# Two out-projections of an encoder by columns instead of rows, norm factors by logarithm and exponential

## The reference

```python
def rmsnorm(x, g, eps=EPS):
    xf = x.astype(jnp.float32)
    xf = xf * lax.rsqrt(jnp.mean(xf * xf, axis=-1, keepdims=True) + eps)
    return (xf * g.astype(jnp.float32)).astype(x.dtype)

# attention, behind the heads; o is (B, S, 8 heads, 128)
o = rmsnorm(o, subln_g, SUBLN_EPS) * (1.0 - lam_init)
o = o.reshape(B, S, D) * jax.nn.silu(z)
return o @ w_out
# Fourier
return (f * jax.nn.silu(z)) @ w_out
# trunk
h = rmsnorm(x, attn_norm);  x = x + diff_attn_branch(h, ...)
h = rmsnorm(x, fnet_norm);  x = x + fourier_branch(h, ...)
return rmsnorm(x, final_norm)
```

## Time and profile before

| | |
|---|---|
| median of 3 runs | 2958.13 us (2956.58 to 2959.44) |
| the profiled execution | 2956.63 us |
| its span in the profile | 2954.8 us, 1.8 us less |
| mean granted TensorE clock | 0.98 of full |
| TensorE busy | 2830.8 us, 96% of the span |
| VectorE, ScalarE, GpSimd busy | 1813.1, 1742.5, 1551.8 us |
| oa | about 2044 to 2302 us |
| of | about 2734 to 2955 us |

### The profile page before, as it was taken

How to read it: one execution, slowest core, us unless ns; L and a number is a source line. 1 busy time by engine, 2 the same in 40 slices (tenths; PEclk the granted TensorE clock), 3 DMA queues, 4 the chain that set the end, 5 groups by cost and what they waited for, 6 DMA issues and landing times. The chain is left out here.

```text
span 2954.8 us, 41608 instructions
## 1 busy us (share of the span) xinstructions
PE 2830.8 (96%) x15126; PEld 2485.9 (84%) x15126; DVE 1813.1 (61%) x2402; ACT 1742.5 (59%) x3126; POOL 1551.8 (53%) x988
## 2 busy tenths in 40 slices
PE   5999999999899999999999999998999899999898
PEld 4999999999688888888888888886788899886687
DVE  7678768766477767677777777776885200441322
ACT  6777777767477777777777777775443311322321
POOL 4556655645265666666566666666563310230642
PEclk8999999999899999999999999999999999999899
DMA  3564554447452314141414131123564522555752
GB/s 112 188 195 139 173 173 149 148 147 204 119 174 79 105 31 107 36 109 36 107 30 109 37 100 46 33 88 115 187 206 165 170 89 78 159 169 200 256 194 98
DMA packets 281815, 374.02 MB, mean 127 GB/s; under 512 B 22923, under 2 KB 258507, under 8 KB 276140
## 3 DMA queue, kind: packets, MB, share of 16 engines
q1 hardware_dynamic: 281484, 371.23, 40.6%
q0 software_dynamic: 128, 0.13, 0.0%
HBM read 258.04 MB, written 125.97 MB: 130 GB/s over the span
## 5 line engine op out<-in xcount | busy, mean ns | idle before, releaser
L1285 DVE TENSOR_REDUCE pa_half_max<-pa_score 128x1 f32<-128x1024 f32 x512 | 624.0, 1219 | 310.4 <-PE pa_score L1055 310.3
L1209 ACT ACTIVATE pa_p<-pa_score,pa_neg_max 128x1024 f32<-128x1024 f32 x512 | 567.8, 1111 | 69.9 <-DVE pa_neg_max L1291 69.8
L1111 PE MATMUL pa_o_acc<-pa_wt,pa_vv 128*128 128x256 f32 x2048 | 507.8, 380 | 1.5 <-ACT pa_o_out_s L1248 1.4
L206 PE MATMUL ia_acc<-ia_xh,ia_wh 128*128 128x384 f32 x1344 | 454.3, 338 | 33.3 <-DVE ia_xl L675 16.0
L451 POOL TENSOR_TENSOR ia_w_sums<-ia_raw 128x512 f32<-128x512 f32 x240 | 334.5, 1397 | 256.5 <-PE ia_acc L208 234.8
L1051 PE MATMUL pa_score<-pa_ka,pa_qa 128*128 128x512 f32 x1024 | 452.1, 442 | 16.3 <-ACT pa_p L1209 8.8
L207 PE MATMUL ia_acc<-ia_xl,ia_wh 128*128 128x384 f32 x1344 | 452.2, 336 | 0.0
L208 PE MATMUL ia_acc<-ia_xh,ia_wl 128*128 128x384 f32 x1344 | 452.1, 336 | 0.0
L1187 ACT ACTIVATE pa_wt<-pa_turned 128x512 f32<-128x512 f32 x512 | 306.2, 598 | 229.1 <-PE pa_turned L1085 221.6
L1055 PE MATMUL pa_score<-pa_kb,pa_qb 96*128 96x512 f32 x1024 | 422.1, 412 | 0.0
L1111 PEld LDWEIGHTS pa_o_acc<-pa_wt,pa_vv 128*128 128x128 f32 x2048 | 367.6, 190 | 46.0 <-ACT pa_o_out_s L1248 3.1
(11 more groups left out here) (286 smaller groups left out, 5245.5 us busy)
## 6 DMA issues: line engine op xcount, KB each, us to landing
ia_raw<-attn_w_in SPq DMA_DIRECT2D x48, 1024.0 KB, 6.3
qk_hi<-ia_hi SPq DMA_DIRECT2D x96, 192.0 KB, 4.9
qk_lo<-ia_c SPq DMA_DIRECT2D x96, 192.0 KB, 2.8
pa_ka<-qk_hi SPq DMA_DIRECT2D x32, 512.0 KB, 8.8
fl_slices<-normed SPq DMA_DIRECT2D x26, 512.0 KB, 6.7
ia_h<-x_cols SPq DMA_DIRECT2D x24, 384.0 KB, 4.1
v<-ia_c SPq DMA_DIRECT2D x48, 192.0 KB, 5.6
attn_gate<-ia_c SPq DMA_DIRECT2D x48, 192.0 KB, 2.0
```

What stands on the lines that cost most here:

```text
L206: pe.matmul(out, a_hi(k), b_hi(k), start=first and n == 0, stop=False)
L1111: mm = pe.matmul(acc, vv[:, k], wt[:, g % 2, k], start=k == 0, stop=k == NB - 1)
L1209: act.activation(dst[:, half * HALF:(half + 1) * HALF], score[:, (4 * q + j) % RING].rearrange("p a b -> p (a b)"), ACT.Exp, bias=neg_max[ ...
L1285: dve.tensor_reduce(half_max[:, q % 2, n, half:half + 1], score[:, (4 * q + j) % RING].rearrange("p a b -> p (a b)"), AX_X, ALU.max).then_ ...
```

## The change

`project_rows` becomes `project_out`, in which everything behind the product stays in columns.

- The weights are the stationary operand and the branch moves: matmuls of 256 columns (a pair's tokens), 1728 per stage. A pair has four quarters `r` of two blocks of output features; `acc` is four PSUM banks, each zeroed by a matmul at the beginning, the first pair being accumulated on these zeros.
- The residual comes in columns (`x_cols`, and `x1` as written by oa), one load of 1 MB per pair into one of two slots; sums and results are stored in two halves per pair.
- The norm over features is now a sum over partitions and blocks: ScalarE squares half a pair (`column_square`, L1705, twice), VectorE sums the 8 blocks (`column_total`, L1797), TensorE sums over the partitions by an fp32 matmul with ones (`total`, L1646), ScalarE makes the factor (`column_factor`, L1711 and L1714), VectorE multiplies in 8 instructions (`scale_out`, L1809). Turns, `take_turned` and the unit matrix are gone. The last pair's sum is made in two parts.
- Every root with its reciprocal, those of the heads (`head_root`, L1691 and L1694) and those of the features, is exp(-0.5 ln(...)) on ScalarE.
- The host turns the final columns into rows.

The diff, cut to its core:

```diff
-def project_rows(nc, tag, w_dram, branch, gate, residual, out, ident_dram=None, subln=None, columns=None, column_norm=None, final_norm=None, first=None, branches=1, ahead=(), columns_last=None, branch_last=None):
+def project_out(nc, tag, w_dram, branch, gate, residual, norm, out, subln=None, sums_out=None, first=None, branches=1, ahead=(), out_last=None, branch_last=None):
...
-        x1 = m.sb("x1", [P, SLOTS, D])
-        row_out = m.sb("row_out", [P, 2, D])
-        acc = m.ps("acc", [P, 2, 2, GROUP])
+        x1 = m.sb("x1", [P, 2, KB, PAIR_T])
...
+        acc = m.ps("acc", [P, QUARTERS_T, GROUP])
+        totals = m.ps("totals", [P, 2, GROUP])
...
+                def load_residual(p):
+                    wait(sp, scaled, KB * (p - 1))
+                    if sums_out is not None:
+                        wait(sp, sums_stored[p % 2], 32 * (p // 2))
+                    sp.dma_start(x1[:, p % 2], residual[:, :, pair_cols(p)].rearrange("k p t -> p k t")).then_inc(res_in[p % 2], 16)
...
-                    store(2 * p - 2)
+                    store_sum(p - 1, 0)
                     for n in range(2 * p + 4, min(2 * p + 6, N_UNITS)):
                         load_unit(n)
-                    for t in range(max(2 * p + 1, SLOTS), min(2 * p + 3, NT)):
-                        load_residual(t)
-                    store(2 * p - 1)
-                    if columns is not None and p >= 2:
-                        store_columns(p - 2)
+                    if p >= 2:
+                        if p < N_PAIRS:
+                            load_residual(p)
+                        store_out(p - 2)
+                    store_sum(p - 1, 1)
...
-                def multiply(t, half, heads=range(KB)):
-                    s, at, cols = (t // 2) % 2, slice((t % 2) * P, (t % 2) * P + P), slice(half * GROUP, (half + 1) * GROUP)
-                    mm = three_pass(pe, acc[:, t % 2, half], lambda k: ah[:, s, k, at], lambda k: al[:, s, k, at],
-                                    lambda k: wh[:, k, cols], lambda k: wl[:, k, cols], heads,
-                                    first=heads[0] == 0, last=heads[-1] == KB - 1)
+                def multiply(p, r, heads=range(KB)):
+
+                    for c in range(2):
+                        cols = slice((2 * r + c) * P, (2 * r + c + 1) * P)
+                        mm = three_pass(pe, acc[:, r, c * PAIR_T:(c + 1) * PAIR_T], lambda k: wh[:, k, cols], lambda k: wl[:, k, cols],
+                                        lambda k: ah[:, p % 2, k], lambda k: al[:, p % 2, k], heads,
+                                        first=p > 0, last=heads[-1] == KB - 1 and (c == 1 or p > 0))
...
+                    for r in range(QUARTERS_T):
+                        pe.wait_ge(added, QUARTERS_T * (p - 2) + r + 1)
+                        multiply(p - 1, r)
+                        if r == 1:
+                            total(p - 2)
+                        if ahead and r % 2 == 1:
+                            sum_squares(2 * p + 2 + r // 2)
+                total(LAST)
...
-                                   ACT.Sqrt, bias=eps[:, 0:1], scale=1.0 / P).then_inc(rooted, 1)
+                                   ACT.Ln, bias=eps[:, 0:1], scale=1.0 / P).then_inc(logged, 1)
+                    act.wait_ge(logged, n + 1 - NORMED)
+                    act.activation(square_slot(n), square_slot(n), ACT.Exp, scale=-0.5).then_inc(rooted, 1)
...
+                def column_factor(p):
+                    act.wait_ge(totalled, p + 1)
+                    wait(act, scaled, KB * (p - 1))
+                    act.activation(factor[:, p % 2], totals[:, p % 2, :PAIR_T], ACT.Ln, bias=eps[:, 1:2],
+                                   scale=1.0 / D).then_inc(total_logs, 1)
+                    act.wait_ge(total_logs, p + 1)
+                    act.activation(factor[:, p % 2], factor[:, p % 2], ACT.Exp, scale=-0.5).then_inc(factors, 1)
...
                 for p in range(2, N_PAIRS + 1):
-                    t = 2 * p - 2
                     ahead = rms and 2 * p + 3 < N_UNITS
+                    column_square(p - 2, 1)
                     if p < N_PAIRS:
                         high(2 * p)
                     if ahead:
                         square(2 * p + 2)
-                    row_norm(t - 1)
-                    scale_rows(t - 1)
+                    column_factor(p - 2)
                     if ahead:
                         head_root(2 * p + 2)
...
+                def column_total(p):
+                    dve.wait_ge(column_squared, 2 * p + 2)
+                    wait(dve, totalled, p - 1)
+                    dve.tensor_reduce(column_sum[:, p % 2], normed[:, p % 2].rearrange("p k t -> p t k"), axis=AX_X, op=ALU.add).then_inc(
+                        column_summed, 1)
...
+                    for k in range(KB):
+                        dve.scalar_tensor_tensor(out=normed[:, p % 2, k], in0=x1[:, p % 2, k], scalar=norm_w[:, k:k + 1],
+                                                 in1=factor[:, p % 2], op0=ALU.mult, op1=ALU.mult).then_inc(scaled, 1)
```

More of the change, by code:

```diff
@@ L1672, in _ @@
                 pe.wait_ge(zeroed, 1)
-                for n in range(2):
-                    pe.matmul(acc[:, 1, 1], zeros[:, :P], zeros, start=True, stop=True)
+                for r in range(QUARTERS_T):
+                    pe.matmul(acc[:, r], zeros[:, :P], zeros, start=True, stop=False)
                 first_pair(0)
                 first_pair(1)
-                if columns is not None:
-                    pe.wait_ge(consts_in, 16 * n_consts)
-                if columns is not None:
-                    turn(0)
@@ L1681, in _ @@
                 for p in range(2, N_PAIRS + 1):
-                    t = 2 * p - 2
                     ahead = rms and 2 * p + 3 < N_UNITS
                     pe.wait_ge(a_lo, 2 * p)
-                    pe.wait_ge(added, 2 * (t - 2) + 1)
-                    multiply(t, 0)
-                    pe.wait_ge(added, 2 * (t - 2) + 2)
-                    multiply(t, 1)
-                    if ahead:
-                        sum_squares(2 * p + 2)
-                    if columns is not None:
-                        turn(t - 1)
@@ L1693, in _ @@
-                    pe.wait_ge(added, 2 * (t - 1) + 1)
-                    multiply(t + 1, 0)
-                    pe.wait_ge(added, 2 * (t - 1) + 2)
-                    multiply(t + 1, 1)
-                    if ahead:
-                        sum_squares(2 * p + 3)
-                    if columns is not None:
-                        turn(t)
-                if columns is not None:
-                    turn(NT - 1)
+                    for r in range(QUARTERS_T):
+                        pe.wait_ge(added, QUARTERS_T * (p - 2) + r + 1)
[4 more added lines that the diff above has]
+                            sum_squares(2 * p + 2 + r // 2)
@@ L1829, in scale_out, with add @@
[L1829 to L1841 removed]
+                def add(p, r):
+                    dve.wait_ge(products, QUARTERS_T * p + r + 1)
+                    if r == 0:
+                        dve.wait_ge(res_in[p % 2], 16 * (p // 2 + 1))
+                    blocks = x1[:, p % 2, 2 * r:2 * r + 2].rearrange("p a b -> p (a b)")
+                    dve.tensor_tensor(blocks, acc[:, r], blocks, ALU.add).then_inc(added, 1)
```

289 lines of the change are left out of this document (109 added, 180 removed).

## The result

The changed kernel takes 2986.68 us as the median of 4 runs (2985.15 to 2989.69), the kernel before 2958.02 us of 4. The ratio is 1.0101 with a 95% interval of 1.0089 to 1.0113, so it is 1% slower. The same kernel timed a second time beside the kernel before (last experiment) gave 1.0093 (1.0079 to 1.0107). The profiled execution took 2985.15 us, its span is 2983.4 us.

The account below looks back on a forecast made before the run. Prediction took TensorE to bound both stages, except at their beginnings and ends. Terms gave oa +5.7 and of +18.9, together +24.6 on 2956.6 us: 2981.2, as a median 2983 us; 8 in 10 between 2965 and 3000.

Parts of the forecast that it names:

- products, each stage: Matmuls in `acc`: two of 256 columns take 11.1 ns more than one of 512; 768 times, +8.5 us per stage.
- turns: oa: turns of eight transposes, 0.88 us each, go; turns 1 to 15 lie between products, -13.2 us.
- totals, each stage: Eight fp32 matmuls of 128x256 per stage come between products, 0.5 us each: +4.0 us per stage.
- stall in oa: Mid-pair, ScalarE and GpSimd's 14.4 us chain outlasts TensorE's 12.5; TensorE waits 1.9 us in six passes: +11 us.
- beginning of oa: Units 2 and 3 need no reciprocals; second pair starts earlier (-4.2) and half clock goes (-1.9): -6.1 us.
- oa's tail: End of oa: old 9.1 us tail becomes 0.9 for the add plus 9.4, and a two-piece store: +1.5 us.
- of's tail: End of of: from last add to last scaling 9.4 us where it took 3.0: +6.4 us (5 to 9).
- of's beginning: of's second pair waits 6.43 us for GpSimd's unchanged low part, covering zeroing matmuls and longer products: 0.
- rival 3: A table switch costs more than its 1.28 us record, in oa's chain and the tails: 3016 us; chance 5%.
- Rival 1: No stall in oa, as overlap and shorter handovers take 1.9 us off the 14.4 us chain: 2972 us; chance 15%.
- Rival 2: oa's six stalls bring the clock down, half-clock matmuls following: +11, 2994 us; decides above about 2.2 us; chance 17%.
- Rival 4: Not slower: the fixed 12 ns per matmul is hidden, 18 us less per stage than in the sum: 2956 us; chance 8%.

Follow-up runs that it names:

- The longer stall: Changed kernel with four copies of 128x512 elements added to ScalarE's chain between factor and heads' root, in six passes of oa: 3011.29 us, ratio 1.019 to the kernel before.
- the version with square roots: Changed kernel with the projections' logarithms and exponentials replaced by square roots on ScalarE and reciprocals on VectorE: 3037.61 us, ratio 1.0275 to the kernel before.

## Why the prediction was right, point by point

The forecast was 2983 us in 2965 to 3000; it is 2986.7. On the profiled execution's own time it was 2981.2 against 2985.15. By the terms of the sum:

| term | predicted | measured |
|---|---|---|
| products, each stage | +8.5 | 1536 x 120.0 against 768 x 226.7 ns: +10.2 |
| turns | -13.2 | 0.92 each: -13.8 |
| totals, each stage | +4.0 | 8 x 0.42: +3.4 |
| stall in oa | +11 | 11.8 less without it |
| beginning of oa | -6.1 | -5.6 start, -1.9 half clock: -7.5 |
| oa's tail | +1.5 | 11.6 to 13.0: +1.4 |
| of's tail | +6.4 | 7.9 to 14.8: +6.9 |
| of's beginning | 0 | -1.0 |
| fg and fl | 0 | +3.0 |

The measured terms add up to +5.5 in oa and +19.5 in of, against +6.2 and +19.5 by the stretches. The misses go both ways: products, the stall and of's tail were put too low; the totals and of's beginning cost less than forecast, and the turns and oa's beginning gave back more. So the sums of the stages are closer than their terms, which is in part luck.

- **Products.** Right in kind, small by a sixth: 120.0 ns instead of the 118.7 of the Fourier stage's rows, and 226.7 instead of 226.3. 1.3 ns count 1536 times a stage. Rounding is not the reason, since 0.01 us over 23 steps is under 1 ns; the single distances in that row of 24 starts scatter from 115 to 135 ns, so a short row of another stage was not a steady one. Read against 2.4 GHz both widths have a fixed part of 13.3 ns. The kernel by rows with halved products shows the term by itself.
- **Stall.** Mechanism, place, count of six and size were right, and taking two of three loads out of the chain removed it. The prediction's text speaks of four loads in the chain in rival 3, while its sum had three; three is right.
- **Rival 1** (no stall) is out: 1.77 us each. **Rival 2** (the clock falls) did not happen in either profile of the changed kernel. The longer stall shows that it was the right fear: of the 25.9 us that it adds in oa, 11 go with the clock. But the 2.2 us that the rival named as its bound does not hold. With the totals made twice the clock fell behind two of six waits of 1.77 us, so that it stayed up in the changed kernel has no cause shown here. **Rival 3** (a switch costs more than its record) is out in this case: behind each of the loads above the activation starts within 0.02 us. The record of the load starts as close behind the activation before it. The drain of 1380 ns that the Trainium skill adds (ScalarE: Activation LUTs, What ACT_TABLE_LOAD costs) doesn't appear in these rows. **Rival 4** (the fixed part is hidden) is out at 120.0 ns.
- **oa's beginning.** The second pair starts 5.6 us earlier, forecast 4.2, although a wait of 1.02 us is left that the forecast had not. The better granted clock ahead of the second pair, 0.91 instead of 0.83, goes with this and was in no term.
- **VectorE.** That the reciprocals cost nothing by rows was right in the steady part; at oa's beginning they cost, as forecast. The prediction priced VectorE's new work by single rows; the reduction took 3.93 us, inside the stated bound of 2.3 to 4.6. That its scalings double beside GpSimd was not foreseen. It cost nothing in the changed kernel, but it is why the expectation for the version with square roots missed by 40 us.
- **The ends.** of's tail is longer by 0.5 us than forecast. The strided reduction has 0.6 of it, and the two totals and the rest give a little back. In the second profile of the changed kernel this tail is 15.7 us instead of 14.8, with the totals at half clock.
- **Not in the sum:** the 3.0 us of fg and fl. They go with a lower granted clock there, and the experiments couldn't tie them to the change. Without them the profiled execution would stand 1 us from the forecast's 2981.2.

## What to carry to other kernels

When products bound a stage, count instructions too: here halving the width cost 6% of a stage's product time, 10.2 us in each of the two stages, while the transposes that went had cost 13.8 us in one of them. A function table is switched in the order that the instructions stand in; put what needs one table together within the chain that the bounding engine waits for, and look at the built order for it. Before a part of a change is kept with the whole, try it alone: here the one piece that paid by a new route, roots without reciprocals at a stage's start, needed none of the rest but a moved turn.

## What the runs showed of the hardware that was not expected

**VectorE beside GpSimd.** Eight scalings of 128x256 with two operands from SBUF, in of of the changed kernel, beside GpSimd's work and without it (VectorE's timeline):

```profile
2795.42 7.55 DVE L1809 SCALAR_TENSOR_TENSOR of_normed<-of_x,of_norm_w,of_factor 128x256 f32<-128x256 f32 x8 [1.98 <-ACT of_factor L1714]
...
2959.64 3.25 DVE L1809 SCALAR_TENSOR_TENSOR of_normed<-of_x,of_norm_w,of_factor 128x256 f32<-128x256 f32 x8 [1.98 <-ACT of_factor L1714]
```

GpSimd's timeline under the first of them:

```profile
2796.48 2.48 POOL L1595 TENSOR_TENSOR of_al<-of_g_more,of_ah 128x1024 fp32r<-128x1024 f32 x1 [8.81 <-ACT of_ah L1699]
2798.92 2.58 POOL L1592 TENSOR_TENSOR of_g_more<-of_b_more,of_g_more 128x1024 f32<-128x1024 f32 x1
```

7.55 us against 3.25. The same is behind the 864 and 508 ns of the two groups of L1809. The reciprocals (6.55 us for two) and the reduction (3.63 to 3.93 us) show no such change. The same instruction's durations in of, by a view of its output's tile (count, shortest, median and longest in ns, first and last start):

```profile
L1809 DVE SCALAR_TENSOR_TENSOR of_normed<-of_x,of_norm_w,of_factor x72: 468/477/2632, 2795.4 to 2978.8; 128x256 f32<-128x256 f32 x72
```

The median is that of the instruction alone; the longest is 2632 ns, 2155 more, while GpSimd's instruction takes 2.48 us. In the eight of the first line two are long: 2.63 us from 2796.62 and 2.62 us from 2799.17, one under each of GpSimd's two instructions, and the other six take 0.47 to 0.49. So single scalings stand still until a GpSimd instruction has ended, and the others run at full speed. The adds, the reciprocals and the reduction have one operand in SBUF. The Trainium skill (SBUF — State Buffer, Who interferes with whom) says that VectorE and GpSimd share a pair of ports as a lock, and that a VectorE instruction with two inputs in SBUF takes it against a GpSimd instruction that reads SBUF. The rows agree. No run here took the lock's cause apart, by an operand in PSUM for instance.

**The clock and the length of a wait.** At one place of one loop, six waits of 4.24 us each were followed by a granted clock of 0.62 to 0.80 in the 8 us behind them, and that cost about 2 us a time. Waits of 1.77 us at the same place left the clock at 1.00 behind all six in the changed kernel, and behind four of six with the totals made twice; behind the other two it was 0.79. In fl a wait of 1.79 us was followed by 0.83 over 27 us. So the length of one wait doesn't decide alone.
